# Fills of the first attention spread by their cost, the next stage's turns and products drawn in, and the recurrence's steps reordered, in a two-block kernel on one Trainium2 core

## The chip, the cores and the metric
One core of one Trainium2 chip runs the whole program. The metric is the device time of one execution, in microseconds (us). Engines are PE (TensorE), DVE (VectorE), ACT (ScalarE), POOL (GpSimd) and SP (SyncE, which here issues nearly all loads). Each works through its own instructions in order and waits on semaphores.

## What is computed
`reference` runs two blocks of two layers on 512 latent tokens of width 1024, all in 32-bit floats, with 256 context tokens beside them in the first block. The change touches the first block alone:
```python
def ab_layer(...):                       # layer 0: attention beside a short convolution
    q, k, v, g_a, xb, b_g, c_g, g_b = split_cols(modulate(x, shift, scale) @ w_in, widths)
    o_a = window_attention(q, k, v, kc, vc, sink)        # context: context_attention
    o_b = b_g * short_conv(c_g * xb, conv_w)
    y = concatenate([o_a * silu(g_a), o_b * silu(g_b)]) @ w_out
    x_new = layer_norm(ALPHA * x + gate * y, ln_g, ln_b)
def hgrn2(...):                          # layer 1: S_t = diag(f_t) S_{t-1} + k_t v_t^T, both directions
    k, log_f = sigmoid(-z), log_sigmoid(z)               # o_t = S_t^T q_t, decays by cumulative sums
```
The conditioning `mod = silu(c) @ w_ada[l] + b_ada[l]` gives shift, scale and gate of each layer; it depends on no token.

## The kernel before
Weights come in chunks of 1 MB through three slots (WSLOTS = 3): SP issues the load of chunk n when PE has released chunk n-3. Products that must be exact in 32 bits are made of three faster ones: ACT rounds a chunk to `weights_hi` (`hi_upto`), POOL subtracts to `weights_lo` (`lo_upto`, in the chunk's own slot), and PE multiplies hi by hi, hi by lo and lo by hi. PE's results go to three PSUM banks in turn (`ring`, `take`): a result needs the bank of the third result before it, as released by DVE ("v") or ACT ("a"). Products of the recurrence go to two further banks.

**First attention** (209.7 to 463 us). 48 units (6 query tiles, 8 heads) run in pairs: scores of both (PE), maxima (DVE), exponentials (ACT), scaling (DVE), turns (PE), their copies (one ACT, one DVE), values (PE). Between scaling and turns PE gets a fill from `AB_FILL`: 24 units of the branch beside the attention (bg, xb, cg; 2 chunks each; 24 matmuls of 512 or 256 columns), one a place over places 0 to 31; then six conditioning chunks of layer 1 (`mod_rows`, `mod_turn`) at places 32 to 37, beside which DVE makes the convolution; then ten of the 16 units of the output product (`y_unit`) at 38 to 47. At the fourth conditioning chunk SP reloads x and ctx (3 MB) in the same queue as the weights. ACT calls `hi_upto` for the next chunk inside a fill.

**Between the layers** (481.3 to 545.7). The context's output product yc0.0 to yc0.3; layer norm of four latent tiles on DVE, whose square root is ACT's `ln_root(1)`, behind `hi_upto("yc0.3")`; `join_part` of yc0.t between its tiles; then `ln_root(2)` for the context; six more conditioning chunks (`mod_run(1, 6, 12)`); turns h1.0 to h1.5 of the normed tiles, which ACT and DVE modulate; the gate row.

**Recurrence** (545.7 to 1122.5). First eight products (z, q, i of head pair 0), then eight steps: head pair hb, direction d = 0 or 1. A step on PE: `dg` (keys by queries, of which DVE keeps the diagonal), `kt` (turns of the decayed keys, which wait for DVE's `hg_ks`), level 0, product slot 0, `su` (state updates), level 1, slot 1, level 2, slot 2, `oi` (states by queries), and levels 3 to 6 with slots 3 to 6 behind them, slot 7 last. In even steps slots 0 to 4 hold products for the next step or head pair (5), in odd ones and the seventh step slots 0 to 5 (6). A level (16 matmuls of 64 columns) needs POOL's `level_args`, ACT's `level_exp` and DVE's `level_operand`. For the next step DVE makes |z| (`abs_z`, behind `across`), ACT exponential and logarithm, DVE `log_f_and_sums` with its scans, all ahead of DVE's operand of level 5; for d = 1 POOL then subtracts (`exclusive`, L2793) before ACT's `state_factors`.

## Time and profile before
| | |
|---|---|
| three runs | 2453.39, 2460.62, 2463.84 us, median 2460.62 |
| the profiled execution's own time | 2457.86 us |
| its span in the profile | 2456.1 us |
| mean granted clock of PE | 0.948 |
| instructions | 27907 |

The span runs from the first to the last instruction recorded; 1.8 us of the execution lie outside it. PE is busy for 91% of the span. From 1122.5 us on (out-projection, second block) nothing is edited.

### The profile page before, as it was taken

Reading aid. Unit: us, or ns where it says so; the run is one execution under the profiler, and the core shown is the slowest. Engines: PE = TensorE matmul, PEld = TensorE weight load, DVE = VectorE, ACT = ScalarE, POOL = GpSimd, SP = SyncE. Lnnn points to the kernel's source line nnn. Section 1 sums busy time; section 2 is a strip of 40 time slices with the busy share of each in tenths; the row PEclk is TensorE's granted clock in tenths of the full one; section 3 lists DMA queues with packets and bytes.
Section 4 is the critical chain, followed back from the end, with each engine's and each line's share of the span. In section 5 each row is a group of like instructions: output and inputs, shape, how many; then the busy total and the mean of one; then the engine's idle time right before and its main releaser. Section 6 shows DMA issues by size and latency. Waiting matters only on the chain. (4 is left out here: it accounts for less than half of the span.)

```text
span 2456.1 us, 27907 instructions
## 1 busy us (share of the span) xinstructions
PE 2243.3 (91%) x11655; PEld 1798.7 (73%) x11655; DVE 1104.9 (45%) x1647; ACT 668.0 (27%) x1030; POOL 835.7 (34%) x393
## 2 busy tenths in 40 slices
PE   5989996978999999999798878999998999999998
PEld 3768885856676767787665667888887767888886
DVE  2023557652556556556996553111116783111113
ACT  3222223223444444453111333010003163010111
POOL 1322102410323323223800024554554345454553
PEclk7999997979999999999899988999999999999999
DMA  9321115351101011112121012332322222232322
GB/s 296 83 72 52 35 35 172 79 163 52 35 23 47 18 35 35 35 52 78 42 65 35 35 35 70 102 103 86 103 92 97 86 86 69 86 103 88 101 95 77
DMA packets 173212, 187.45 MB, mean 76 GB/s; under 512 B 25552, under 2 KB 151840, under 8 KB 172960
## 3 DMA queue, kind: packets, MB, share of 16 engines
q1 hardware_dynamic: 165520, 178.56, 23.1%
q10 hardware_dynamic: 6992, 5.01, 0.7%
q8 instruction: 93, 1.52, 0.3%
q0 software_dynamic: 576, 2.10, 0.2%
q14 instruction: 31, 0.25, 0.0%
HBM read 183.56 MB, written 2.10 MB: 76 GB/s over the span
## 5 line engine op out<-in xcount | busy, mean ns | idle before, releaser
L2816 POOL TENSOR_TENSOR weights_lo<-weights_raw,weights_hi 128x2048 fp32r<-128x2048 f32 (+1 forms) x104 | 471.0, 4528 | 849.5 <-ACT weights_hi L1334 637.6
L646 PE MATMUL ring<-input_hi,weights_hi 128*128 128x512 f32 x784 | 305.4, 390 | 0.0
L648 PE MATMUL ring<-input_hi,weights_lo 128*128 128x512 f32 x784 | 305.0, 389 | 0.0
L647 PE MATMUL ring<-input_lo,weights_hi 128*128 128x512 f32 x784 | 305.0, 389 | 0.0
L2653 DVE CAST weights_hi<-weights_raw 128x2048 fp32r<-128x2048 f32 (+1 forms) x72 | 88.8, 1233 | 378.6 <-PE ring L648 173.9
L2807 POOL TENSOR_TENSOR h_w<-h_p 128x512 f32<-128x512 f32 x56 | 70.3, 1256 | 448.1 <-PE ring L935 367.6
L908 PE MATMUL obank<-acts,weights_raw 128*128 128x512 f32 x384 | 175.2, 611 | 0.8 <-issue 0.8
L646 PEld LDWEIGHTS ring<-input_hi,weights_hi 128*128 128x128 f32 x784 | 147.2, 188 | 31.1 <-issue 0.5
L648 PEld LDWEIGHTS ring<-input_hi,weights_lo 128*128 128x128 f32 x784 | 147.2, 188 | 30.6
L647 PEld LDWEIGHTS ring<-input_lo,weights_hi 128*128 128x128 f32 x784 | 147.2, 188 | 30.5 <-issue 0.2
L919 PE MATMUL obank<-weights_raw,acts 128*128 128x256 f32 x640 | 145.4, 387 | 0.0
L935 PEld LDWEIGHTS ring<-h_w 128*128 128x128 f32 x896 | 114.9, 205 | 32.7 <-issue 19.7
L1246 PE MATMUL ring<-weights_hi,hidden_hi 128*128 128x512 f32 x352 | 136.9, 389 | 0.0
L1247 PE MATMUL ring<-weights_lo,hidden_hi 128*128 128x512 f32 x352 | 136.9, 389 | 0.0
L1248 PE MATMUL ring<-weights_hi,hidden_lo 128*128 128x512 f32 x352 | 136.9, 389 | 0.0
L908 PEld LDWEIGHTS obank<-acts,weights_raw 128*128 128x128 f32 x384 | 73.6, 196 | 86.5 <-issue 86.4
L935 PE MATMUL ring<-h_w 128*128 128x64 f32 x896 | 116.1, 286 | 22.2 <-DVE h_w L2138 8.6
L919 PEld LDWEIGHTS obank<-weights_raw,acts 128*128 128x128 f32 x640 | 122.6, 194 | 17.1 <-issue 0.5
L2674 DVE TENSOR_TENSOR f_gate<-f_gate,ring 128x1024 f32<-128x1024 f32 x22 | 26.9, 1221 | 210.9 <-PE ring L648 210.9
L2921 POOL TENSOR_TENSOR hidden_lo<-f_gate,hidden_hi 128x1024 fp32r<-128x1024 f32 x22 | 52.6, 2390 | 160.8 <-ACT hidden_hi L1786 160.8
L1556 ACT ACTIVATE h_w<-h_w 128x1024 f32<-128x1024 f32 x56 | 59.0, 1056 | 147.6 <-POOL h_w L2808 147.5
L646 PE MATMUL ring<-ab_in_hi,weights_hi 128*128 128x512 f32 (+1 forms) x224 | 78.9, 352 | 17.3 <-POOL ab_in_lo L2823 9.5
(457 smaller groups left out, 4459.2 us busy)
## 6 DMA issues: line engine op xcount, KB each, us to landing
weights_raw<-in_w_ada SPq DMA_DIRECT2D x24, 1024.0 KB, 7.2
weights_raw<-in_ffn_w_gate SPq DMA_DIRECT2D x22, 1024.0 KB, 5.2
weights_raw<-in_ffn_w_up SPq DMA_DIRECT2D x22, 1024.0 KB, 5.2
weights_raw<-in_w_in_c SPq DMA_DIRECT2D x20, 1024.0 KB, 5.1
weights_raw<-in_ffn_w_down SPq DMA_DIRECT2D x16, 1024.0 KB, 4.9
weights_raw<-in_w_in_ab SPq DMA_DIRECT2D x9, 1024.0 KB, 5.2
weights_raw<-in_ev_w_in SPq DMA_DIRECT2D x8, 1024.0 KB, 5.8
weights_raw<-in_od_w_in SPq DMA_DIRECT2D x8, 1024.0 KB, 5.8
```

The lines of the kernel that those rows point to most:

```text
L646: pe.matmul(o, hi[:, k, ms], xh[:, k, t0:t0 + n], start=k == 0, stop=False)
L647: pe.matmul(o, hi[:, k, ms], xl[:, k, t0:t0 + n], start=False, stop=False)
L648: last = pe.matmul(o, lo[:, k, ms], xh[:, k, t0:t0 + n], start=False, stop=k == KD - 1)
L908: last = pe.matmul(ps[:, 0:L], wv[:, k, part * P:(part + 1) * P], HT[:, k, 0:L], start=k == 0, stop=k == KD - 1)
L919: last = pe.matmul(ps[:, j * WC:(j + 1) * WC], HT[:, k, t * P:(t + 1) * P], wv[:, k, :], start=k == 0, stop=k == KD - 1)
L935: last = pe.matmul(ps[:, j * 64:(j + 1) * 64], wt, rv[:, :, 1 - d, :], start=True, stop=True)
L1246: pe.matmul(o, F_HI[f // 2][:, f % 2, ts], hi[:, k, :], start=f == 0, stop=False, skip_group_check=True)
L1247: pe.matmul(o, F_HI[f // 2][:, f % 2, ts], lo[:, k, :], start=False, stop=False, skip_group_check=True)
L1248: last = pe.matmul(o, F_LO[f // 2][:, f % 2, ts], hi[:, k, :], start=False, stop=end, skip_group_check=True)
L2653: dve.tensor_copy(w_hi[:, 0:kt, :], WR[:, slot, 0:kt, :]).then_inc(done, 1)
L2807: pool.tensor_tensor(w4[:, :, :, 0, :], ref, p4[:, :, :, 0, :], ALU.subtract)
L2816: pool.tensor_tensor(W_LO[slot][:, 0:kt, :], WR[:, slot, 0:kt, :], w_hi[:, 0:kt, :], ALU.subtract).then_inc(sem("w_lo"), 1)
```

## The change
- `AB_FILL` is built from a list with a cost for each unit and put at the 24 even places, several units to a place. Conditioning chunks 0 to 8 (nine, MOD_FIRST = 9) stand one behind each weight chunk. Worked out from the code, the places read: bg 0 to 10, xb 12 to 22, cg 24 to 32, the y units from 34; conditioning chunks at 4, 10, 16, 22, 28, 34, 38, 42, 46. At 28: last unit of cg0, chunk 4, first of cg1. At 34: `x_again`, chunk 5, y(0,0). At 38: chunk 6, y(1,0). At 42: y(1,3), chunk 7, y(2,0). At 46: y(2,3), chunk 8, y(3,0). Three y units are left behind the attention.
- The convolution part follows each cg unit on DVE. x and ctx are reloaded from ACT's queue in five transfers (`x_again`). `y_hi` moves into the fills. `hi_upto("y0.0")` comes at the first unit of cg1.
- Between the layers `ln_root(1)` stands ahead of `hi_upto("yc0.3")`; h1.0 to h1.3 come before the last three conditioning chunks, and the first two z products before h1.4, h1.5 and the gate row.
- In the recurrence `dg` is made once a head pair, in the odd step behind `su`, from the sum of both directions' keys (`keys_of_both`). The product slots are 0, 1, 2, 4, 7 (five) or 0, 1, 2, 3, 5, 7 (six); the last step keeps its own. For d = 1 the scans yield the exclusive sums, and POOL's `exclusive` goes. The query operand moves out of `state_operands`. Before step 0 ACT takes only i(0,0) ahead of `state_factors(0)`.

```diff
-            return units + [None] * (8 - len(units))
+            places = range(8) if st == LAST else (0, 1, 2, 4, 7) if len(units) == 5 else (0, 1, 2, 3, 5, 7)
+            placed = dict(zip(places, units))
+            return [placed.get(i) for i in range(8)]
...
-        AB_STEPS = 32
+        Y_UNITS = [("y", c, t) for c in range(4) for t in range(TL)]
+        Y_AFTER = Y_UNITS[-3:]
+        MOD_FIRST = 9
+        a_woven = []
+        for nm, c, x, m in AB_UNITS:
+            a_woven.append((nm, c, x, m))
+            if (nm, c, x) == ("cg", 1, 1):
+                a_woven += [("y_hi", 2 * m), ("y_hi", 2 * m + 1)]
+            if (nm, c, x, m) == ("cg", 1, 1, 1):
+                a_woven.insert(-2, ("x_again",))
+            if (x, m) == (1, 1):
+                a_woven.append(("mod", sum(u[0] == "mod" for u in a_woven)))
+        for unit in Y_UNITS[:-3]:
+            a_woven.append(unit)
+            if unit[2] == TL - 1:
+                a_woven.append(("mod", sum(u[0] == "mod" for u in a_woven)))
+        a_woven.append(("last_mod",))
...
+        def fill_cost(unit):
+            if unit[0] in ("y_hi", "last_mod", "x_again"):
+                return 0
+            return 2 * KD if unit[0] == "mod" else 3 * KD * (2 if unit[0] != "y" and unit[2] == 0 else 1)
...
+        A_PLACES = 24
+        a_costs = [fill_cost(u) for u in a_woven]
         AB_FILL = {}
-        for u, unit in enumerate(AB_UNITS):
-            AB_FILL[u * AB_STEPS // len(AB_UNITS)] = unit
-        MOD_FIRST = 6
-        for j in range(MOD_FIRST):
-            AB_FILL[AB_STEPS + j] = ("mod", j)
-        Y_UNITS = [("y", c, t) for c in range(4) for t in range(TL)]
-        Y_WOVEN = 48 - AB_STEPS - MOD_FIRST
-        for u in range(Y_WOVEN):
-            AB_FILL[AB_STEPS + MOD_FIRST + u] = Y_UNITS[u]
-        Y_AFTER = Y_UNITS[Y_WOVEN:]
-        mod_no = {}
+        for u, unit in enumerate(a_woven):
+            place = min(A_PLACES - 1, A_PLACES * (2 * sum(a_costs[:u]) + a_costs[u]) // (2 * sum(a_costs)))
+            AB_FILL.setdefault(2 * place, []).append(unit)
...
                     if unit[1]:
                         mod_turn(1, unit[1] - 1)
                     mod_rows(1, unit[1])
+                    return
+                if unit[0] == "last_mod":
+                    mod_turn(1, MOD_FIRST - 1)
+                if unit[0] in ("y_hi", "last_mod", "x_again"):
                     return
                 if unit[0] == "y":
                     y_unit(*unit[1:])
...
                 last.then_inc(filled, 1)
                 used_with_unit()
+            for t in range(TL):
+                pe.wait_ge(sem("x1_ready"), t + 1)
+                turn_tiles("h1.", X, (t,), "va"[t % 2])
             mod_run(1, MOD_FIRST, 12)
...
                 return
-            for t in range(6):
-                pe.wait_ge(sem("x1_ready"), t + 1)
-                turn_tiles("h1.", X, (t,), "va"[t % 2])
-            gate_rows(1, 1)
-            pe.wait_ge(*read_of("h1.4"))
-            pe.wait_ge(*read_of("h1.5"))
+            pe.wait_ge(*read_of("h1.2"))
+            pe.wait_ge(*read_of("h1.3"))
...
-            for kind in "zqi":
+            product(("z", 0, 0))
+            product(("z", 0, 1))
+            for t in (4, 5):
+                pe.wait_ge(sem("x1_ready"), t + 1)
+                turn_tiles("h1.", X, (t,), "va"[t % 2])
+            gate_rows(1, 1)
+            pe.wait_ge(*read_of("h1.4"))
+            pe.wait_ge(*read_of("h1.5"))
+            product(("z", 0, 2))
+            for kind in "qi":
                 for part in range(C_PARTS[kind]):
...
-                K_, Q_, I_ = HK[b], HQ[q], HI[q]
+                Q_, I_ = HQ[q], HI[q]
...
-                pe.wait_ge(sem("hg_k"), st + 1)
-                pe.wait_ge(*product_emptied(("q", hb, 1)))
-                ps = take(f"dg{st}", "v")
-                for j in range(TL * HH):
-                    ch, h = divmod(j, HH)
-                    last = pe.matmul(ps[:, j * P:(j + 1) * P], K_[:, h, ch * P:(ch + 1) * P],
-                                     Q_[:, h, ch * P:(ch + 1) * P], start=True, stop=True)
-                last.then_inc(filled, 1)
...
+                    last.then_inc(filled, 1)
+                if d:
+                    pe.wait_ge(*product_emptied(("q", hb, 1)))
+                    pe.wait_ge(sem("hg_k_both"), hb + 1)
+                    ps = take(f"dg{st}", "v")
+                    for j in range(TL * HH):
+                        ch, h = divmod(j, HH)
+                        last = pe.matmul(ps[:, j * P:(j + 1) * P], HK[0][:, h, ch * P:(ch + 1) * P],
+                                         Q_[:, h, ch * P:(ch + 1) * P], start=True, stop=True)
                     last.then_inc(filled, 1)
...
                     sp.wait_ge(*released[n - WSLOTS])
-                if n == mod_no[1, 3]:
-                    sp.wait_ge(*fill_of("cg1.11"))
-                    sp.dma_start(X[:, 0:TL, :], a["x"][0].rearrange("(t p) n -> p t n", p=P)).then_inc(sem("x_in"), 16)
-                    sp.dma_start(X[:, TL:6, :], a["ctx"][0].rearrange("(t p) n -> p t n", p=P)).then_inc(sem("x_in"), 16)
...
                 ts = slice(qt * P, (qt + 1) * P)
-                act.wait_ge(sem("conv"), 8)
+                act.wait_ge(sem("conv"), 6 if qt < TL else 8)
                 act.wait_ge(sem("A_normed"), qt + 1)
...
-                    if unit[1] == MOD_FIRST - 1:
-                        hi_upto("y0.0")
+                elif unit[0] == "last_mod":
+                    mod_columns(1, MOD_FIRST - 1)
+                elif unit[0] == "x_again":
+                    act.wait_ge(*fill_of("cg1.11"))
+                    for c in range(4):
+                        cs = slice(c * WC, (c + 1) * WC)
+                        act.dma_start(X[:, 0:TL, cs], a["x"][0][:, cs].rearrange("(t p) n -> p t n", p=P)).then_inc(sem(f"x_again{c}"), 16)
+                    act.dma_start(X[:, TL:6, :], a["ctx"][0].rearrange("(t p) n -> p t n", p=P)).then_inc(sem("ctx_again"), 16)
+                elif unit[0] == "y_hi":
+                    y_hi(unit[1])
                 elif unit[0] == "y":
-                    if unit[1:] == (0, 0):
-                        mod_columns(1, MOD_FIRST - 1)
                     if unit[2] == 0:
                         hi_upto(f"y0.{unit[1] + 1}" if unit[1] < 3 else "yc0.0")
-                elif unit[2:] == (0, 0) and unit[:2] != ("cg", 1):
-                    hi_upto(names[names.index(f"{unit[0]}{unit[1]}") + 1])
-            attention("A", APB, APT, 0.125, True, lambda i: y_hi(i - 36) if 36 <= i < 40 else None, woven)
+                elif unit[2:] == (0, 0):
+                    hi_upto((names + ["y0.0"])[names.index(f"{unit[0]}{unit[1]}") + 1])
+            attention("A", APB, APT, 0.125, True, lambda i: None, woven)
             for qt in range(4, 6):
                 y_hi(qt)
             for unit in Y_AFTER:
                 woven(unit)
-            hi_upto("yc0.3")
...
-            ln_root(1, 0, 4)
-            ln_root(2, 4, 6)
-            mod_run(1, MOD_FIRST, 12)
-            for t in (1, 3, 5):
+            def h1_tile(t):
                 act.wait_ge(*fill_of(f"h1.{t}"))
                 j = 0 if t < TL else 1
                 for k in range(KD):
                     ins = act.activation(HT[:, k, t * P:(t + 1) * P], bank(f"h1.{t}")[:, k * P:(k + 1) * P], ACT.Identity,
...
                 ins.then_inc(emptied["a"], 1)
+            hi_upto("yc0.2")
+            ln_root(1, 0, 4)
+            hi_upto("yc0.3")
+            h1_tile(1)
+            h1_tile(3)
+            mod_run(1, MOD_FIRST, 12)
+            ln_root(2, 4, 6)
...
-            act.wait_ge(*fill_of("gate1.0"))
-            ps = bank("gate1.0")
-            act.activation(GT[:, 0, :], ps[:, :], ACT.Copy).then_inc(emptied["a"], 1)
...
                     act.wait_ge(sem("hg_w"), 7 * (st - 1))
+                if st >= 2 and st % 2 == 0:
+                    act.wait_ge(*fill_of(f"dg{st - 1}"))
...
-                    act.wait_ge(sem("hg_excl"), STEPS[st][0] + 1)
...
-            for part in range(3):
-                take_product(("z", 0, part))
+            take_product(("z", 0, 0))
+            take_product(("z", 0, 1))
+            h1_tile(5)
+            act.wait_ge(*fill_of("gate1.0"))
+            ps = bank("gate1.0")
+            act.activation(GT[:, 0, :], ps[:, :], ACT.Copy).then_inc(emptied["a"], 1)
+            take_product(("z", 0, 2))
             keys(0)
             log1p_exp(0)
             for part in range(2):
                 take_product(("q", 0, part))
-            for part in range(3):
-                take_product(("i", 0, part))
+            take_product(("i", 0, 0))
             state_factors(0)
             level_exp(0)
             level_exp(1)
+            take_product(("i", 0, 1))
+            take_product(("i", 0, 2))
...
-                if unit[0] == "mod":
-                    if unit[1] < 4:
-                        for x in range(2):
-                            conv_part(unit[1], x)
+                if unit[0] in ("mod", "y_hi", "last_mod", "x_again"):
                     return
                 if unit[0] == "y":
                     _, c, t = unit
-                    if c == 0 and t == 0:
-                        dve.wait_ge(sem("x_in"), 64)
+                    if t == 0:
+                        dve.wait_ge(sem(f"x_again{c}"), 16)
                     join_part(f"y0.{c}.{t}", c, t, 1, ATMP)
                     return
...
                 dve.wait_ge(*read_of(label))
+                if nm == "cg":
+                    conv_part(i, x)
...
+            dve.wait_ge(sem("ctx_again"), 16)
             layer_norm(1, "x1", 0, 4, 32, lambda t: join_part(f"yc0.{t}", t, 4, 2, ATMP))
+            modulated(1, "h1.", (0, 2))
             layer_norm(2, "x1", 4, 6, 32)
...
-            modulated(1, "h1.", (0, 2, 4))
+            modulated(1, "h1.", (4,))
...
-                for h in range(HH):
-                    dve.tensor_tensor_scan(HP[b][:, h, 0:L], tab("chunk"), HT_[b][:, h, 0:L], 0.0, ALU.mult, ALU.add)
-                    last = dve.tensor_tensor_scan(HP[b][:, h, L:LT], tab("chunk", 0, LC), HT_[b][:, h, L:LT], 0.0, ALU.mult, ALU.add)
-                link(last)
-                link(dve.tensor_copy(PL[b], HP[b][:, :, :].rearrange("p h (c t) -> p h c t", t=P)[:, :, :, P - 1]))
+                ends = [v[:, :, :].rearrange("p h (c t) -> p h c t", t=P)[:, :, :, P - 1] for v in (HP[b], HT_[b])]
+                if STEPS[st][1] == 0:
+                    for h in range(HH):
+                        dve.tensor_tensor_scan(HP[b][:, h, 0:L], tab("chunk"), HT_[b][:, h, 0:L], 0.0, ALU.mult, ALU.add)
+                        last = dve.tensor_tensor_scan(HP[b][:, h, L:LT], tab("chunk", 0, LC), HT_[b][:, h, L:LT], 0.0, ALU.mult, ALU.add)
+                    link(last)
+                    link(dve.tensor_copy(PL[b], ends[0]))
+                else:
+                    if st == 1:
+                        dve.memset(HP[b][:, :, 0:1], 0.0)
+                        link(dve.memset(HP[b][:, :, L:L + 1], 0.0))
+                    for h in range(HH):
+                        dve.tensor_tensor_scan(HP[b][:, h, 1:L], HT_[b][:, h, 0:L - 1], tab("chunk", 1, L), 0.0, ALU.add, ALU.mult)
+                        last = dve.tensor_tensor_scan(HP[b][:, h, L + 1:LT], HT_[b][:, h, L:LT - 1], tab("chunk", 1, LC), 0.0, ALU.add, ALU.mult)
+                    link(last)
+                    link(dve.tensor_tensor(PL[b], ends[0], ends[1], ALU.add))
                 dve.tensor_copy(DEC[b], PL[b]).then_inc(sem("hg_sums"), 1)
...
             def state_operands(st):
-                b, q = st % 2, STEPS[st][0] % 2
+                b = st % 2
                 dve.wait_ge(sem("hg_k"), st + 1)
                 dve.wait_ge(sem("hg_exps"), st + 1)
                 dve.tensor_tensor(HZ[b][:, :, :], HZ[b][:, :, :], HK[b][:, :, :], ALU.mult).then_inc(sem("hg_ks"), 1)
+            def query_operand(st):
+                b, q = st % 2, STEPS[st][0] % 2
                 dve.wait_ge(*product_emptied(("q", STEPS[st][0], 1)))
                 dve.tensor_tensor(HT_[b][:, :, 0:L], HT_[b][:, :, 0:L], HQ[q][:, :, :], ALU.mult).then_inc(sem("hg_qi"), 1)
...
                 dve.wait_ge(*fill_of(f"dg{st}"))
                 src = bank(f"dg{st}")[:, :].rearrange("p (j c) -> p j c", j=TL * HH)
-                idb = IDENT.unsqueeze(1).to_broadcast([P, TL * HH, P])
-                S = HSC[hb % 2]
-                if d == 0:
-                    dve.tensor_tensor(S[:, :, :], src, idb, ALU.mult).then_inc(emptied["v"], 1)
-                    dve.wait_ge(*read_of(f"dg{st}"))
-                else:
-                    dve.tensor_tensor(HDG[:, :, :], src, idb, ALU.mult).then_inc(emptied["v"], 1)
-                    dve.wait_ge(*read_of(f"dg{st}"))
-                    link(dve.tensor_tensor(S[:, :, :], S[:, :, :], HDG[:, :, :], ALU.add))
+                own = IDENT.bitcast(U32).unsqueeze(1).to_broadcast([P, TL * HH, P])
+                dve.copy_predicated(HSC[STEPS[st][0] % 2][:, :, :], own, src).then_inc(emptied["v"], 1)
+                dve.wait_ge(*read_of(f"dg{st}"))
+            def keys_of_both(hb):
+                k0, k1 = HK[0][:, :, 0:L], HK[1][:, :, 0:L]
+                dve.wait_ge(sem("hg_k"), 2 * hb + 2)
+                dve.tensor_tensor(k0, k0, k1, ALU.add).then_inc(sem("hg_k_both"), 1)
...
+                dve.wait_ge(*product_emptied(("q", hb, 1)))
                 level_operand(7 * st)
-                diagonal(st)
                 level_operand(7 * st + 1)
+                if d:
+                    keys_of_both(hb)
                 level_scores(st, 0)
                 if d == 0 and hb:
                     inside(hb - 1)
+                query_operand(st)
                 states(st)
+                if d:
+                    diagonal(st)
...
                         lo_upto("y10.0")
                     if more:
-                        exclusive(st + 1)
                         pool.wait_ge(sem("hg_sums"), st + 2)
```

## Rows read from the trace of the kernel before

**Rows 1.** The page, busy time of each engine over the span.
```profile
PE 2243.3 (91%) x11655; PEld 1798.7 (73%) x11655; DVE 1104.9 (45%) x1647; ACT 668.0 (27%) x1030; POOL 835.7 (34%) x393
```
**Rows 2.** Windows: stretch, length, busy us of PE, PEld, DVE, ACT, POOL; clock, DMA.
```profile
209.70:378.00 168.30, 158.74 (x1289) 136.85 (x1288) 92.36 (x219) 49.31 (x103) 22.94 (x5) 1.00 0.13 42
378.00:420.00 42.00, 22.84 (x200) 14.66 (x197) 33.32 (x70) 17.62 (x47) 7.07 (x3) 0.65 0.77 239
420.00:481.30 61.30, 58.48 (x477) 54.97 (x478) 38.44 (x75) 14.12 (x30) 30.70 (x9) 0.96 0.21 53
481.30:545.70 64.40, 50.88 (x365) 42.13 (x364) 42.86 (x69) 20.52 (x49) 13.81 (x3) 0.79 0.59 180
...
870.00:936.60 66.60, 62.61 (x287) 44.82 (x287) 42.06 (x46) 30.30 (x35) 21.70 (x15) 0.90 0.10 32
936.60:999.20 62.60, 60.96 (x334) 49.78 (x335) 36.33 (x44) 26.17 (x36) 17.42 (x14) 1.00 0.11 34
```
**Rows 3.** Waits of PE, 209.7 to 545: total us, times, longest.
```profile
PE ring L707 <- ACT mod_rows L1357: 5.9, 1, 5.9
...
PE ring L821 <- DVE a_tmp L1894: 3.7, 2, 3.5
PE ring L740 <- ACT a_probs_t L1445: 2.7, 8, 0.3
```
**Rows 4.** Timeline of PE near 379 and 524: start, us, instruction.
```profile
379.10 1.07 PE L698 MATMUL ring<-weights_raw,silu_cond 128*32 128x256 f32 x16
...
524.28 1.93 PE L698 MATMUL ring<-weights_raw,silu_cond 128*32 128x256 f32 x16
...
527.09 1.93 PE L698 MATMUL ring<-weights_raw,silu_cond 128*32 128x256 f32 x16
```
**Rows 5.** DMA issues near 381 and 456: count, KB each, us to landing.
```profile
weights_raw<-in_w_ada SPq DMA_DIRECT2D x1, 1024.0 KB, 13.8
...
weights_raw<-in_w_out_ab SPq DMA_DIRECT2D x1, 512.0 KB, 5.1
```
**Rows 6.** Timeline of ACT, 482 to 524.
```profile
487.78 1.92 ACT L1334 ACTIVATE weights_hi<-weights_raw 128x2048 fp32r<-128x2048 f32 x1 [4.37 <-DMA weights_raw<-in_w_out_ab]
...
497.65 0.21 ACT L1481 ACTIVATE small<-small 128x4 f32<-128x4 f32 x1
520.01 0.20 ACT L1481 ACTIVATE small<-small 128x2 f32<-128x2 f32 x1 [22.16 <-DVE small L1907]
```
**Rows 7.** Timeline of PE at the recurrence's first step.
```profile
600.93 1.95 PE L984 MATMUL ring<-h_q,h_k 128*128 128x128 f32 x16
609.62 2.40 PE L993 MATMUL ring<-tables,h_z 128*128 128x128 f32 x10 [6.75 <-DVE h_z L2125]
613.18 3.65 PE L935 MATMUL ring<-h_w 128*128 128x64 f32 x16 [1.17 <-DVE h_scores L2149]
616.62 8.41 PE L908 MATMUL obank<-acts,weights_raw 128*128 128x512 f32 x16
```
**Rows 8.** Timeline of PE in the fifth and sixth steps.
```profile
905.31 7.09 PE L908 MATMUL obank<-acts,weights_raw 128*128 128x512 f32 x16
...
923.19 7.09 PE L935 MATMUL ring<-h_w 128*128 128x64 f32 x32 [2.14 <-DVE h_w L2138]
...
936.56 1.97 PE L935 MATMUL ring<-h_w 128*128 128x64 f32 x16 [1.85 <-DVE h_diag L2152]
...
975.35 1.89 PE L935 MATMUL ring<-h_w 128*128 128x64 f32 x16
...
999.22 1.97 PE L935 MATMUL ring<-h_w 128*128 128x64 f32 x16 [1.66 <-DVE h_scores L2149]
```
**Rows 9.** Timeline of DVE in the same two steps.
```profile
908.24 1.52 DVE L2138 TENSOR_TENSOR h_w<-h_w,h_q 128x512 f32<-128x512 f32 x1
...
919.22 3.91 DVE L2138 TENSOR_TENSOR h_w<-h_w,h_q 128x512 f32<-128x512 f32 x1
...
982.33 0.68 DVE L2138 TENSOR_TENSOR h_w<-h_w,h_k 128x512 f32<-128x512 f32 x1
```

More of the change, by code:

```diff
@@ L226, in program @@
         HKT = [view(gt_at + D, 4 * HH, P, name="h_kt"), view(xc + 1280, HH, P, name="h_kt")]
-        HDG = view(bc_at + D, TL * HH, P, name="h_diag")
         HO = view(hi_at, TL, D, name="h_out")
@@ L490, in program @@
                   22: ("ev", 1, 3), 26: ("em", 0), 28: ("em", 1), 30: ("em", 2)}
+        E_FILL = {i: [unit] for i, unit in E_FILL.items()}
         E_WOVEN = 3
@@ L691, in mod_rows @@
             def mod_rows(l, j):
-                mod_no[l, j] = len(chunks)
                 wv = chunk(cols(a["w_ada"][l], j * WC))
@@ L733, in attention @@
                     if what == "fill":
-                        fill(FILLS[kind][i])
+                        for unit in FILLS[kind][i]:
+                            fill(unit)
                     elif what == "scores" and i % 2 == 0:
@@ L828, in y_unit @@
                 if t == 0:
-                    if c == 0:
-                        mod_turn(1, MOD_FIRST - 1)
                     parts_of["y", c] = split_chunk(f"y0.{c}", head_rows(c))
@@ L1420, in attention @@
                     if what == "fill":
-                        fill(FILLS[kind][i])
+                        for unit in FILLS[kind][i]:
+                            fill(unit)
                     elif what == "scores":
@@ L2034, in attention @@
                     if what == "fill":
-                        fill(FILLS[kind][i])
+                        for unit in FILLS[kind][i]:
+                            fill(unit)
                     elif what == "scores":
```

7 lines of the change are left out of this document (removed).

## The prediction
> **What bounds the kernel now.** I read the page first: PE is busy 91% of the span [rows 1], no other engine comes near half. So the time is PE's work, its idle time, and stretches in which it works at the lower clock. Next I read windows over the three edited places [rows 2]. In the attention PE idles 9.6 us up to 378, 19.2 in 378:420, 2.8 after: 31.5 in all. The middle window, where the conditioning chunks stand in a row, has a clock of 0.65 and DMA engines busy for 0.77: it waits for weights. Between the layers (481:546) it idles 13.5 at a clock of 0.79. In the recurrence PE is nearly full: step 4 (870 to 936.6) idles 4, step 5 1.6. Then the waits [rows 3]: 5.9 and 3.5 us are single waits between the layers, the 0.3 us waits those of the attention's pairs. Last the timelines [rows 4, 6 to 9], to see what is late behind each wait.
>
> The sum is made against the profiled execution's own time, 2457.86; the median of three is 2.76 above. In the timelines an operation's duration overlaps the next by 0.15 to 0.2 (a level at 613.18 lasts 3.65, the product behind starts at 616.62 [rows 7]), so I take a level as 1.75 at full clock and 3.5 at half, a product as 6.95 and, begun at the low clock, 8.2.
>
> **A. Attention, 209.7 to 481.3.** Three more conditioning chunks come in: 1.07 of products at full clock [rows 4] and about 0.4 of turns, 1.5 each, +4.5. The idle of before goes: -31.5. Its low clock goes: a clock of 0.65 over 22.8 busy us is 8, the 0.96 later 2.3, and some 1.7 of turns: -12.
>
> New stalls: ACT's `hi_upto` for the next chunk is called in the fill directly behind a conditioning chunk (places 28, 34, 38, 42, 46). That load needs the slot three chunks back, which the last unit of the weight chunk before releases, and at these five places that unit stands in the same fill or the one just ahead. So the load starts while ACT already waits for it, and ACT's exponentials and copies for the pair are queued behind. A 512 KB piece takes 5.1 [rows 5]; with two issues ahead of the last piece I estimate 1.3 more, 6.4; `hi` 1.92 [rows 6] and ACT's copies of the pair follow. Less what PE has of its own in the fill: 2.6 at 28, 5.4 at 38, 6.5 at 42, 3.3 at 46. At 34 the 3 MB of x and ctx run beside it from ACT's queue. The rows give two bounds for the load: 6.4 alone, 13.8 for a chunk that landed behind the same 3 MB [rows 5]. Two queues sharing lie between; I take the middle, 10.1, and the stall is 7.5 (3.8 to 11.2). Sum +25.3. Each stall is followed by low clock over some 2 to 2.5 us of lost work; five make +11 (bounds 0 and 17, were each to cost one operation of 7 at 8.2 and two levels at 3.5). In the fills without stall each pair still waits about 0.34 for ACT's `a_probs_t`, as 8 pairs do now [rows 3]; 19 more: +6.5. Moving the convolution parts behind the cg units adds nothing to DVE, which is busy 92 of 168 us here [rows 2]; would it not hide, 8 parts would go on the pairs' maxima. A: 4.5 - 31.5 - 12 + 25.3 + 11 + 6.5 = **+3.8**.
>
> What the row shows of the shared load is only a chunk behind 3 MB in one queue, 13.8 [rows 5]. The Trainium skill (DMA: Bandwidth & Descriptors, "Queues, rings and completion order") says that an engine takes turns between its queues packet by packet; by this estimate the chunk would take about 9.4 and the stall 0.7 less. No row of before has two such queues side by side.
>
> **B. Between the layers.** `ln_root(1)` now stands behind a `hi` that needs a chunk in the middle of the row; before, it stood behind `hi` of yc0.3, whose load came 4.37 late [rows 6]. DVE's statistics of the norm are done near 489, the root ran at 497.65; I put it at 490.9, so the normed tiles come 6.8 earlier. With it go PE's waits of 5.9 and 3.5 [rows 3]: -9.4. Three conditioning chunks leave the row where they cost 2.8 each (524.28 to 527.09 [rows 4]): -8.4. Low clock beside them: -2.4. New: h1.2 waits for the join of yc0.3, h1.3 for the bank that DVE frees behind h1.0: estimated 4.8, between 0 (DVE keeps pace) and 9.4 (the wait only changes its name). The context's tiles h1.4, h1.5 stand behind two z products of 7 each, which cover `ln_root(2)` (520.01, after 22 us of waiting for DVE [rows 6]); without that cover it would be some 6. B: -9.4 - 8.4 - 2.4 + 4.8 = **-15.4**.
>
> **C. Start of the recurrence.** ACT takes i(0,0) alone before `state_factors(0)`, so DVE's operand is there near 596 where PE needs it at 601. The waits of 6.75 and 1.17 go [rows 7], `dg` of step 0 (1.95, 1.8 net) goes, and the low clock that follows the wait: `kt` 1.1, level 0 1.8, product 1.3. C: **-13.9**.
>
> **D. The steps.** I walk step 4 with the slots 0, 1, 2, 4, 7. PE reaches level 4 at 905.3 (no product in slot 3), but DVE's operand ends at 909.8 [rows 8, 9]: an idle 4.5. Then level 4 at the low clock 3.5, product 8.2, levels 5 and 6 3.5, product 6.95, `kt` 1.1: the next level 0 at 933.1, where it was 936.56 [rows 8]. That is -3.5; the old wait of 2.14 and the low clock of the two levels (7.09 for both [rows 8]) are in it, and the gone subtraction on POOL, beside which DVE's 0.68 took 3.91 [rows 9]. Steps 0 and 2 walked in the same way give -2.4 and -3.1. Together -9.0.
>
> Step 5 has the slots 0, 1, 2, 3, 5, 7. Level 5 stands right behind level 4, PE is free at 977.1, the operand of level 5 ends at 983.0 [rows 8, 9], because |z| and the scans of the next step still stand ahead of it: an idle 5.9. Then level 3.5, product 8.2, level 1.75, product 6.95, `kt` 1.1: 1004.5 instead of 999.22, +5.3. Its `dg` stays, 1.8, and level 1 waits 0.4 for the bank of `su`; the product after level 0 no longer meets a low clock, -1.0 on average. So +6.5, three times: +19.5. The seventh step has the wait of step 5 and no `dg`: -0.5; the last keeps its slots and has its `dg`, 1.8 + 0.4: +2.2. D: -9.0 + 19.5 - 0.5 + 2.2 = **+12.2**. The sum of keys (one DVE operation of about 0.7), `copy_predicated` for a product and the shifted scans (same lengths) lie beside PE's products and are costed at nothing; were the cover gone, they would be 0.7 a step. ACT's `keys` of the next even step now waits for `dg` of the odd step; `dg` is made in the first third of the step and the keys are made in its second half, so nothing is late behind it.
>
> **Sum.** +3.8 - 15.4 - 13.9 + 12.2 = -13.3: 2444.6 for the profiled execution, **2447** against the median.
>
> **Rivals.**
> *Slower: clock lost behind each empty slot.* Where levels stand without a product between them, the clock stays low not for one level but through the next and its product. For it: the two levels at 923.19 took 7.09, both at half speed after a wait of only 2.14 [rows 8]. Against it: in step 5 the same order of work keeps a clock of 1.00 [rows 2]. It would add one level and most of a product, about 4 us, in each of seven steps: +28, 2475. The change is slower than before from +1.9 a step, by over 0.5% from +3.7. The Trainium skill (TensorE: Matmul & The Clock Gate, Part 1) says that micro-idles between groups of matmuls make the clock swing between its two levels; by that this rival would hold.
>
> *The attention's fills do not stall.* If the slot is released soon enough, or the load is less than 6.4, the 25.3 and 8 of the 11 of low clock go: 2414. For it: in the first 168 us, with the same calls of `hi_upto`, PE idles just 9.6 [rows 2]. Against: there no conditioning chunk takes a slot in between.
>
> *The shifted slots are better than walked.* The next step's chain starts earlier because products come earlier in ACT's order, and the operand of level 5 with it. The odd steps' idle and low clock go (19) and half of the even steps' idle (6): 2422. Against: DVE's order before level 5 is the same.
>
> *No change.* The root stays as late as before since `hi_upto("yc0.2")` itself waits for its load; B loses its 9.4: 2457.
>
> **How the numbers follow.** Forecast 0.45, its own range 2439 to 2455 (the bounds of the load at 34, of the low clock and of the 4.8). Slower rival 0.12, no stalls 0.15, better slots 0.13, no change 0.15. The range reaches to 2418, between the two faster rivals, and to 2468, short of the slower one; outside lie about two thirds of 0.15 and of 0.12. A measurement of this kernel tells about 0.5% (12.3 us) from no change. Faster than 2448.3 are the two fast rivals (0.28) and somewhat over half of the forecast (0.25): 0.53. Slower than 2472.9: most of the slow rival (0.11) and 0.03 of the forecast's tail: 0.14. Within: 0.33.
>
> **What would show it.** A: in the changed profile ACT waits for DMA of the weights at places 28, 34, 38, 42 and 46, 3 to 8 us of PE idle at each, and no stretch with a clock of 0.65 for 40 us. If PE idles under 15 there, the load term is wrong. B: `ln_root(1)` within 9 us of the last y unit; the 5.9 is absent. If ACT still waits over 4 for a load ahead of the root, the fourth rival holds. C: `kt` begins directly behind the third i product. D: PE waits on `h_w` before level 4 in even steps (4 to 5) and before level 5 in odd ones (about 6); four `dg` instead of eight; nothing of L2793 on POOL. Even steps under 63.1, odd ones near 69. If the levels behind the empty slots take 3.5 each and the product behind them 8 or more in all steps, the slower rival holds. The prediction would be wrong above all if several conditioning chunks wait at PE itself for their load, which I cost at nothing, since the slot of each is free well before its place.

## The result and the profile after

Four runs of the changed kernel, beside four of the kernel before: 2478.80 us median (2477.32 to 2484.11) against 2460.46 (2453.39 to 2463.84), ratio 1.0089, 95% interval 1.0072 to 1.0106. The change makes the kernel slower by 0.9%. 2447 with a range of 2418 to 2468 was predicted. The profiled span went from 2456.1 to 2477.4, +21.3.

The page's busy times, the row that answers [rows 1]:
```profile
PE 2234.0 (90%) x11591; PEld 1791.5 (72%) x11591; DVE 1086.7 (44%) x1645; ACT 667.8 (27%) x1029; POOL 826.8 (33%) x389
```
PE is busy 9 us less and the span is 21 longer, so its idle time rose by 31. Windows of the changed kernel (columns as in [rows 2]); the second ends where the three y units behind the attention are done, as 481.3 did before, the third behind the third z product, as 566.5 did:
```profile
209.70:378.00 168.30, 151.99 (x1265) 130.22 (x1264) 100.46 (x224) 51.21 (x110) 22.80 (x5) 0.98 0.23 70
378.00:514.60 136.60, 96.41 (x754) 86.23 (x755) 59.27 (x138) 33.06 (x80) 36.98 (x11) 0.81 0.31 85
514.60:588.40 73.80, 63.80 (x374) 47.63 (x373) 47.16 (x72) 20.44 (x42) 13.80 (x3) 0.88 0.38 115
```
The attention's stretch takes 304.9 us instead of 271.6, +33.3; PE idles 56.5 of them, 31.5 before, and is busy 248.4, 240.1 before. The stretch between the layers takes 73.8 instead of 85.2, -11.4. What PE waited for from 209 to 560, total us, times, longest, against [rows 3]:
```profile
PE ring L759 <- ACT a_probs_t L1471: 38.6, 20, 12.7
PE obank L781 <- ACT a_probs_t L1471: 5.2, 1, 5.2
PE obank L781 <- issue: 3.9, 2, 2.3
PE ring L707 <- DVE a_tmp L1933: 3.7, 2, 2.9
PE obank L781 <- DVE a_probs_t L2113: 3.1, 2, 2.4
```
The 5.9 us of ACT's `mod_rows` is gone. The largest waits are now for ACT's copy of the turned probabilities. The longest case, place 34, in the timelines of PE and of ACT (start, us, instruction, idle before it in brackets with what ended it):
```profile
426.01 1.22 PE L759 MATMUL ring<-a_kv,a_q 64*128 64x128 f32 x8 [12.66 <-ACT a_probs_t L1471]
```
```profile
412.42 0.38 ACT L1382 ACTIVATE mod_rows<-ring 128x256 f32<-128x256 f32 x1
423.69 1.91 ACT L1359 ACTIVATE weights_hi<-weights_raw 128x2048 fp32r<-128x2048 f32 x1 [10.89 <-DMA weights_raw<-in_w_out_ab]
425.50 0.37 ACT L1471 ACTIVATE a_probs_t<-ring 128x256 f32<-128x256 f32 x1
```
ACT stands 10.9 us at `hi_upto("y0.1")`, and a copy of 0.37 us, for which PE waits, is queued behind it. The five waits of this kind are 6.2, 12.7, 5.7, 7.2 and 5.2 us (places 28, 34, 38, 42, 46). The load's issues from 407 to 411 (count, KB, us to landing):
```profile
resid<-in_x ACTq DMA_DIRECT2D x4, 512.0 KB, 7.3
resid<-in_ctx ACTq DMA_DIRECT2D x1, 1024.0 KB, 14.6
weights_raw<-in_w_out_ab SPq DMA_DIRECT2D x2, 256.0 KB, 9.8
weights_raw<-in_w_out_ab SPq DMA_DIRECT2D x1, 512.0 KB, 13.9
```
Between the layers and at the start of the recurrence, PE's timeline of the changed kernel. Its last two rows answer [rows 7]: `kt` has no wait, `dg` is gone:
```profile
542.85 1.06 PE L707 MATMUL ring<-tables,resid 128*128 128x128 f32 x8 [0.79 <-DVE a_tmp L1933]
546.81 1.94 PE L707 MATMUL ring<-tables,resid 128*128 128x128 f32 x8 [2.90 <-DVE a_tmp L1933]
550.22 1.94 PE L707 MATMUL ring<-tables,resid 128*128 128x128 f32 x8 [1.46 <-DVE acts L1924]
...
559.41 17.05 PE L927 MATMUL obank<-acts,weights_raw 128*128 128x512 f32 x32 [1.15 <-DMA weights_raw<-in_w_in_c]
...
622.67 1.26 PE L1013 MATMUL ring<-tables,h_z 128*128 128x128 f32 x10
623.77 1.90 PE L954 MATMUL ring<-h_w 128*128 128x64 f32 x16
```
And one odd and one even step, against [rows 8]:
```profile
858.18 1.90 PE L954 MATMUL ring<-h_w 128*128 128x64 f32 x16
865.90 3.67 PE L954 MATMUL ring<-h_w 128*128 128x64 f32 x16 [5.83 <-DVE h_w L2193]
869.38 8.82 PE L938 MATMUL obank<-weights_raw,acts 128*128 128x256 f32 x32
878.03 1.90 PE L954 MATMUL ring<-h_w 128*128 128x64 f32 x16
...
925.86 3.67 PE L954 MATMUL ring<-h_w 128*128 128x64 f32 x16 [4.34 <-DVE h_w L2193]
929.33 9.53 PE L927 MATMUL obank<-acts,weights_raw 128*128 128x512 f32 x16
938.70 3.68 PE L954 MATMUL ring<-h_w 128*128 128x64 f32 x32
```
The waits foretold, 5.9 before level 5 and 4.5 before level 4, stand there as 5.83 (four times) and 4.34 (three times).

The whole difference by stretch: attention +33.3; between the layers -11.4; from there to the first level 0 -11.3 (35.4 instead of 46.7); from it to the last level +14.0 (521.3 instead of 507.3); the unedited rest -3.3. Sum +21.3. No run tries the edits between the layers by themselves; their -11.4 is read from these windows.

### The profile page after: what moved, and what is told of

Same layout as the page of the kernel before. It is cut to its first block and busy times, and to the rows that moved or that the text cites. A ratio compares the mean times of both kernels' runs of the same rounds, so it can differ in the third digit from the quotient of the medians.

```text
span 2477.4 us, 27765 instructions
## 1 busy us (share of the span) xinstructions
PE 2234.0 (90%) x11591; PEld 1791.5 (72%) x11591; DVE 1086.7 (44%) x1645; ACT 667.8 (27%) x1029; POOL 826.8 (33%) x389
```

## The experiments

The theory after the result: the attention's loss comes from ACT waiting for a load that was issued only a few us before, and the recurrence's from the empty slots. Each ratio is to runs of the kernel before made beside it (medians 2456.9 to 2460.2).

**Old slots.**
```diff
-            places = range(8) if st == LAST else (0, 1, 2, 4, 7) if len(units) == 5 else (0, 1, 2, 3, 5, 7)
+            places = range(8)
```


> The changed kernel with the recurrence's product slots as they were (0 to 4, or 0 to 5); all else stays. Theory (the empty slots cost: PE waits 4.34 before level 4 in three even steps and 5.83 before level 5 in four odd ones, and runs a level and a product at the low clock behind each): those waits go, some 2 us come back before levels 5 and 6 of the even steps, and the recurrence becomes shorter than before by 5 to 15 us instead of longer by 17. Expected 2452 us, 2446 to 2457. Rival (the time is lost to the new order of dg, keys and scans, not to the slots): 2476 to 2482.


Measured 2463.58, ratio 1.0021 (1.0012 to 1.0030): 15.2 us off the changed kernel, where 27 were expected. The seven waits of 4.3 and 5.8 us went, but behind the even steps 0, 2 and 4 the next `kt` now waits 4.3 to 4.5:
```profile
800.64 3.68 PE L954 MATMUL ring<-h_w 128*128 128x64 f32 x32
808.62 2.39 PE L1013 MATMUL ring<-tables,h_z 128*128 128x128 f32 x10 [4.29 <-DVE h_z L2176]
811.17 1.11 PE L954 MATMUL ring<-h_w 128*128 128x64 f32 x4 [0.16 <-DVE h_w L2193]
```
The slots are a cause, the rival falls. But of the even steps only step 0 gets shorter (56.6 for 60.4 from `kt` to `kt`); steps 2 and 4 take 62.4 and 64.1, in the changed kernel 62.4 both, since PE gets to `kt` sooner and waits there for the keys. And in steps 2, 4, 6 and 7 level 0 now waits 2.3 us for its operand, with low clock behind it:
```profile
877.56 3.27 PE L954 MATMUL ring<-h_w 128*128 128x64 f32 x16 [2.26 <-DVE h_w L2193]
880.62 9.21 PE L927 MATMUL obank<-acts,weights_raw 128*128 128x512 f32 x16
```

**ACT rounds one unit later.**
```diff
-                    if unit[2] == 0:
+                    if unit[2] == 1:
                         hi_upto(f"y0.{unit[1] + 1}" if unit[1] < 3 else "yc0.0")
-                elif unit[2:] == (0, 0):
+                elif unit[2:] == (0, 1):
```


> The changed kernel, but ACT rounds the next weight chunk one unit later (at the second unit of a chunk and not at its first). Theory (ACT stands in front of a load that was issued only some 2 us before, and the pair's exponentials and copies are queued behind it): of the 36.9 us of PE waits at places 28, 34, 38, 42 and 46 at least 30 go, and some 8 of low clock with them. Expected 2440 us, 2434 to 2448. Rival (the loads are late for PE too, so that the wait moves to the next chunk's first product): 2470 or more, with new waits on weights_lo in the attention.


Measured 2450.41, ratio 0.9969 (0.9954 to 0.9984): 28.4 off the changed kernel. PE's waits from 209 to 486:
```profile
PE obank L781 <- DVE a_probs_t L2113: 10.4, 6, 2.9
PE ring L759 <- ACT a_probs_t L1471: 7.1, 20, 0.6
PE obank L781 <- issue: 4.1, 3, 2.3
```
```profile
209.70:485.60 275.90, 246.60 (x2039) 214.47 (x2037) 163.95 (x364) 84.24 (x190) 60.33 (x16) 0.96 0.30 85
```
All five long waits are gone and none on `weights_lo` over 1.4 took their place; the attention fell from 304.9 to 275.9. That settles the mechanism. 10 us are short of the expectation: PE's idle time fell by 27.2 (56.5 to 29.3) and not by the 36.9 of the five waits, because others grew, DVE's copies from 3.1 to 10.4; and PE's busy time fell by 1.8, where some 8 of low clock were expected.

**x in quarters**, each ahead of its output chunk, ctx at the end:
```diff
+                if unit[0] == "y" and unit[2] == 2:
+                    if unit[1] < 3:
+                        x_columns(unit[1] + 1)
+                    else:
+                        act.dma_start(X[:, TL:6, :], a["ctx"][0].rearrange("(t p) n -> p t n", p=P)).then_inc(sem("ctx_again"), 16)
...
                     act.wait_ge(*fill_of("cg1.11"))
-                    for c in range(4):
...
+                    x_columns(0)
```


> The changed kernel, but x is reloaded one quarter at a time (0.5 MB ahead of each output chunk) and ctx at the end, in place of 3 MB at once at place 34. Theory (two queues share the engines, so the chunk for y0.1 took 15.2 us from issue to landing beside 3 MB): the chunk lands in 7 to 9 us, the wait of 12.7 at place 34 falls to 5 or 6, the others stay. Expected 2471 us, 2467 to 2474. Rival (the chunk is late because of the conditioning chunk issued just ahead, not of x): 2476 to 2482.


Measured 2469.99, ratio 1.0046 (1.0031 to 1.0061), 8.8 off. Issues near place 34, and PE's wait there:
```profile
weights_raw<-in_w_out_ab SPq DMA_DIRECT2D x2, 256.0 KB, 4.0
weights_raw<-in_w_out_ab SPq DMA_DIRECT2D x1, 512.0 KB, 5.0
```
```profile
415.69 0.84 PE L759 MATMUL ring<-a_kv,a_q 64*128 64x128 f32 x8 [4.19 <-ACT a_probs_t L1471]
```
The last piece landed after 5.0 instead of 13.9 and the wait is 4.2 instead of 12.7: the 3 MB make most of it, not the conditioning chunk, which still stands ahead.

**x in one queue with the weights**, the same five transfers issued by SP directly ahead of the chunk for y0.1 and no longer by ACT:
```diff
+                if n == split_chunks[split_no["y0.1"]]:
+                    sp.wait_ge(*fill_of("cg1.11"))
+                    for c in range(4):
...
+                    sp.dma_start(X[:, TL:6, :], a["ctx"][0].rearrange("(t p) n -> p t n", p=P)).then_inc(sem("ctx_again"), 16)
```


> The changed kernel with its five reloads of x and ctx in SP's queue, directly ahead of the chunk for y0.1, instead of in ACT's queue beside it. Theory (two queues side by side move less: 257 GB/s on average over 408 to 424.3 in the changed kernel, with 180 to 290 in the middle where both are at work, and 340 to 420 with one): 4 MB at some 370 GB/s take 11.5 us, the chunk lands near 420 in place of 423.7, the wait at place 34 falls from 12.7 to 9 or 10, time 2476 us, 2472 to 2479. Rival (the transfers of x are slow in either queue, or the chunk gains from sharing): the chunk lands at 424 or later, the wait is 12 or more, time as the changed kernel's or above.


Measured 2482.39, ratio 1.0102 (1.0081 to 1.0123). The last piece landed 13.2 us after its issue at 410.2, at 423.4 (423.7 in the changed kernel). But x was issued 1.5 us earlier here (405.93 against 407.45), so the chunk landed 17.5 us after the first transfer of x where it took 16.2, and PE's wait is longer:
```profile
425.74 1.22 PE L759 MATMUL ring<-a_kv,a_q 64*128 64x128 f32 x8 [16.36 <-ACT a_probs_t L1477]
```
The rival holds: sharing between two queues is not what costs. What the 4 MB lack is rate: 240 GB/s in one queue (405.9 to 423.4) and 251 in two (407.5 to 424.2). Why the last 5 us before 421 move only 163 to 248 GB/s here, where 340 to 420 flowed from 412 to 416, stays open. It may be in part the chunk's own: with nothing beside it, in the kernel with x in quarters, it moved 216 GB/s in its middle (410 to 411.5). The chunk behind 3 MB in the kernel before ([rows 5], 13.8) was one of `w_ada`, and it moved at 328 to 365.

**All three edits.**


> The three edits together on the changed kernel: old slots, ACT's rounding one unit later, x reloaded in quarters. Theory: the gains of the first two add (27 and 39), of the third most is already in the second. Expected 2411 us, 2403 to 2420, faster than before by 1.6 to 2.3 per cent. Rival (the waits are one chain and the gains overlap, or DVE becomes late in the attention): 2430 or more.


Measured 2434.81, ratio 0.9894 (0.9874 to 0.9915): 44 off the changed kernel, 25 faster than before. The attention takes 271.0 us with three conditioning chunks more than before:
```profile
209.70:480.70 271.00, 244.56 (x2027) 212.35 (x2025) 162.80 (x364) 84.59 (x190) 60.40 (x16) 0.96 0.29 86
```
The sum of the three gains is 52.4, so 8 are missing, and the time is the rival's (2430 or more). Up to the last level of the recurrence, where no unedited part enters, the traces say the same: 16.3, 31.5 and 12.9 us for the single edits, 60.7 in all, and 51.6 for the three together (1093.4 against 1145.0). The gains overlap by 9: beside the first two, x in quarters brings 3.8 and not 12.9, as the theory had it: with the rounding later, the wait at place 34 is gone already. The unedited rest is no part of this: over the thirteen profiled kernels it varied from 1332 to 1340, and the changed kernel's own was the shortest.

**The recurrence alone**, on the kernel before: all edits from the last i product on, with shifted and with old slots; and **the shifted slots alone** on the kernel before.


> The kernel before with the change's edits from the last i product on alone (order before step 0, dg once a head pair, exclusive scans, shifted slots); attention and the stretch between the layers as before. Theory (the parts add; in the changed kernel's trace the start of the recurrence is 11.3 us shorter and the steps 13.9 us longer, 3.1 of low clock counted in the steps): 2463 us, 2459 to 2467. Rival (the steps depend on how they are reached, so that the parts do not add): outside of that.

> The same without the shifted slots. Theory: the start keeps its 11.3 us, the steps are as long as in the run with old slots, 2.3 us under those of before, so 2447 us, 2443 to 2451; dg once a head pair saves three dg of 1.8 us, and kt then waits for its keys instead (4.3 to 4.5 in each even step). Rival (dg once saves what it weighs): 2441 or less.

> The kernel before with the shifted slots alone. Theory (each odd step waits 5.8 us before level 5 and runs a level and a product at the low clock; in even steps the wait only changes its place): slower by 12 to 20 us, 2476 us. Rival (the shift costs only beside the new order of dg and keys): within 5 us of before.


Measured 2462.51 (ratio 1.0019, 1.0008 to 1.0030), 2445.49 (0.9948, 0.9932 to 0.9964) and 2492.29 (1.0140, 1.0122 to 1.0158). The first two came as expected: the parts add. The third was off: the shift alone costs 34.9, twice the expectation. Worked out from the starts of `kt` in the traces (us from one `kt` to the next):

| kernel | steps 0 to 6 | first `kt` to last level |
|---|---|---|
| before | 64.9, 63.3, 64.3, 64.9, 66.4, 62.8, 68.6 | 510.8 |
| slots alone | 68.7, 70.0, 65.5, 70.5, 68.9, 70.8, 75.5 | 542.5 |
| new order, shifted slots (changed) | 60.4, 70.6, 62.4, 70.7, 62.4, 70.7, 70.9 | 522.4 |
| new order, old slots | 56.6, 66.1, 62.4, 66.7, 62.4, 67.0, 64.9 | 504.7 |

The third row is the changed kernel, whose attention differs too, but the steps do not feel it: the recurrence alone gives 522.7 for its 522.4. The fourth is the recurrence alone. The new order (`dg` once, no `exclusive`) is worth 20 us under the shifted slots and 6 under the old ones. Part of it is seen in step 6 of the slots alone, PE and DVE:
```profile
1080.71 3.68 PE L937 MATMUL ring<-h_w 128*128 128x64 f32 x16 [9.13 <-DVE h_w L2140]
```
```profile
1076.15 0.69 DVE L2140 TENSOR_TENSOR h_w<-h_w,h_k 128x512 f32<-128x512 f32 x1
1076.75 3.91 DVE L2140 TENSOR_TENSOR h_w<-h_w,h_q 128x512 f32<-128x512 f32 x1
```
POOL's `exclusive` runs beside the second operation, from 1076.3 to 1080.1, and it takes 3.91 ([rows 9] has the same); in the recurrence alone, without `exclusive`, it takes 0.69. With old slots a product covers most of it, and PE waits 2.14 [rows 8]; with an empty slot PE waits 9.13 instead of 5.83. The odd steps are 5.6 to 8 us longer, step 6 is 6.9 and the other even ones are 1.2 to 3.8; what makes up the even steps' part beyond this operation was not tried by itself.

**The convolution behind the copies**, on the kernel with three edits: DVE keeps the part in a list and makes it after it has copied the pair's turned probabilities:
```diff
                 if nm == "cg":
-                    conv_part(i, x)
+                    conv_later.append((i, x))
...
                         dve.tensor_copy(PT[:, i % 2, 0:nb * P], ps[:, 0:nb * P]).then_inc(emptied["v"], 1)
+                        while conv_later:
+                            conv_part(*conv_later.pop(0))
```


> The kernel with all three edits, and each convolution part moved on DVE behind the copy of the pair's turned probabilities. In the kernel with three edits PE waits 9.4 us, 6 times, for DVE's copy of the turned probabilities, at the places of the cg units. Theory (DVE does the convolution first, and the copy is queued behind it): those waits go, some low clock with them, 2424 us, 2420 to 2430. Rival (the convolution then delays the next pair's maxima and the wait only moves): 2432 to 2438.


Measured 2432.01, ratio 0.9894 (0.9875 to 0.9914), the ratio of the kernel with three edits. The rival holds: the convolution is what makes DVE late, and it does so in either place. PE's waits from 209 to 486 have changed their names:
```profile
PE ring L768 <- DVE a_probs L2114: 6.6, 2, 5.1
PE ring L716 <- ACT a_probs L1457: 4.1, 1, 4.1
PE obank L781 <- DVE a_probs_t L2122: 3.5, 3, 2.5
PE ring L878 <- ACT a_probs L1457: 3.0, 1, 3.0
```
With the parts behind the copies it is the next pair's maxima and scaling that come late, where it was the copies before.

**Factors first**, on the kernel with three edits:
```diff
                 level_exp(7 * st + 6)
-                between(4)
                 if more:
                     state_factors(st + 1)
+                between(4)
```


> The kernel with three edits, and in each step ACT's state_factors for the next step ahead of its taking the product of slot 4. In the kernel with three edits the sums for step 3 are ready at 762.9, but ACT begins the factors at 765.9, behind the product of slot 4, and kt waits 4.29 us for what follows from them. Theory: kt's wait falls by 2 to 3 us in each of four even steps, and the low clock behind it in part: 2425 us, 2421 to 2430. Rival (ACT's factors delay the product's bank or the level exponentials by as much): 2433 to 2437.


Measured 2423.42, ratio 0.9866 (0.9841 to 0.9891). ACT and PE at the end of step 2, first in the kernel with three edits, then here:
```profile
765.28 0.60 ACT L1551 ACTIVATE h_q<-obank 128x512 f32<-128x512 f32 x1 [1.86 <-PE obank L927]
765.90 1.28 ACT L1582 ACT_TABLE_LOAD   x1
767.19 0.21 ACT L1582 ACTIVATE small<-small 128x12 f32<-128x12 f32 x1
```
```profile
773.06 2.39 PE L1013 MATMUL ring<-tables,h_z 128*128 128x128 f32 x10 [4.29 <-DVE h_z L2183]
```
```profile
760.54 0.21 ACT L1582 ACTIVATE small<-small 128x12 f32<-128x12 f32 x1 [0.82 <-DVE small L2177]
```
```profile
768.46 2.40 PE L1013 MATMUL ring<-tables,h_z 128*128 128x128 f32 x10 [2.09 <-DVE h_z L2183]
```
ACT's exponentials begin as soon as DVE's sums are there, with no copy and no table load (1.28 us, between two functions) ahead of them, and `kt`'s wait falls from 4.29 to 2.09. Up to the last level 8.5 us are gained. This is the fastest kernel of the study, 34.7 us under the kernel before.

**All five.**


> Three edits, the convolution behind the copies, and the factors first. Theory: the two gains add, 2414 us, 2408 to 2422. Rival (one of the two does nothing): 2423 or more.


Measured 2427.74, ratio 0.9880 (0.9859 to 0.9901). The rival holds. The convolution's place adds nothing, as it did alone; the median is even 4.3 above factors first, but the runs overlap (2424.89 to 2431.39, 2421.15 to 2427.58).

## Why the prediction was wrong

**A is the step that failed: +3.8 predicted, +33.3 measured.** The stalls that it named came, by its mechanism, at the five places. What failed is the size of three terms: the stalls (11.6 us short), the idle time that was to go (13.1 short) and the low clock that was to go (4.8 short).
- Stalls, 25.3 predicted, 36.9 measured. By place: 28, 2.6 and 6.2; 34, 7.5 and 12.7; 38, 5.4 and 5.7; 42, 6.5 and 7.2; 46, 3.3 and 5.2. At 34 I took the middle between 6.4 and 13.8 for the load. It took 13.9 for the last piece and 15.3 from the first issue, past the upper bound: the chunk lands with the end of the 3 MB (423.7, 424.2), not halfway. The estimate that I drew from the Trainium skill (DMA: Bandwidth & Descriptors, "Queues, rings and completion order"), 9.4, was further off still. The trace agrees with the turns: from 413 to 417.5 the two queues moved 543 and 506 packets. But both together moved 230 GB/s there, where the chunk behind 3 MB in the kernel before moved at 328 to 365, so the turns did not bring it in sooner. At 28 the last piece took 8.6 behind the conditioning chunk issued 1.4 us before it, where I had 5.1.
- The rest of the idle, 6.5 predicted, 19.6 measured (56.5 less 36.9). I subtracted all of the 31.5 us of before and gave back one kind of wait, the small ones for ACT's copies. Those came as forecast, 6.9. The other 12.7 are waits that I had at nothing: DVE's copies 4.0, DVE's taking of the fills' results 3.1, ACT's of the conditioning 1.2, 3.9 for which the profile shows no cause, and smaller ones. The convolution was costed at nothing; with the stalls out of the way, DVE's late copies are 10.4 us, and the one other place tried for it cost the same. The sentence that named where it would fall if the cover were gone was there, but without a price, and nothing of it entered the sum or the range.
- Low clock and busy time: 243.6 us of PE's work predicted (240.1 + 4.5 - 12 + 11), 248.4 measured. The clock of 378:514.6 is 0.81, which over 96 busy us is 18, reckoned as I reckoned the 8 of before. But not much of it hangs on the five stalls: without them, with ACT rounding later, PE is still busy 246.6 at a clock of 0.96. So it is less the 11 that were too few than the 12 of before that did not go; PE still idles 29 us there, in shorter waits.

**B: -15.4 predicted, -11.4 measured.** The root came 10.1 us after the first context product began (524.69 against 514.6), 16.4 before, so 6.3 earlier where I had 6.8; the new waits of h1.1 to h1.3 are 5.15 for 4.8. What was missing is the clock behind them: the two z products took 17.05 where 13.97 was their time before, and a load is late by 1.15. My sign for the "no change" rival, ACT waiting over 4 us for a load ahead of the root, was there (4.35), and the rival did not hold: ACT was through with that chunk at 523.4, when DVE's statistics had only just ended (522.9), so the load cost the root 1.8 us at most.

**C and D.** Of the 13.9 in C, 3.1 are low clock behind the first level 0, which the boundary used above counts in the steps. Cut so, C is -10.8 predicted and -11.3 measured, D +9.1 predicted and +14.0 measured. The waits were right to 0.2 us (4.34 and 5.83 for 4.5 and 5.9), odd steps 70.7 for 69. Two things were short. The product behind the empty slot takes 8.6 to 9.4 from its start to the next instruction's instead of 8.2, seven times, 5.8 in all. And the seventh step, which I had 0.5 shorter, is 2.3 longer (70.9 for 68.6). Against them, even steps are 60.4 and 62.4, for 63.1 in step 4, and the last step grew by half a us for 2.2.

**The rivals.** "Slower, clock lost behind each empty slot" gave 2475, near the 2479 measured, but for a reason that is not there: after the wait one level and one product are slow, and the levels behind them run at full clock again (3.68 for two, 938.70 above), so that it adds to the walk 0.8 us a step, 6 of its 28. The swing between the two levels that the Trainium skill names for micro-idles (TensorE: Matmul & The Clock Gate, Part 1) is seen in this case's traces, behind waits of 2.1 and 2.3 us too: the two levels at 923.19 of the kernel before [rows 8], the level and product at 877.56 with old slots. It does not last as long as the rival had it. "No stalls" did not hold in the changed kernel; made true by moving ACT's rounding, it gave 2450, not 2414: the attention took 275.9 where this rival comes to 242.1, with 29.3 of idle for 6.5 and 246.6 busy for 235.6. "Better slots" was wrong: the operand's chain did not move. "No change" was wrong in its mechanism.

From -13.3 to +21.3 is 34.6: A 29.5 (11.6 stalls, 13.1 idle, 4.8 low clock), B 4.0, C -0.5, D 4.9, the rest -3.3. The range took the bounds of single terms (the load, the clock) and had none for its largest term, "-31.5 idle goes". Had 19.6 been left of it, with DVE busy 92 of 168 us [rows 2] a reason to, the forecast would have been near 2460; with the load at its upper bound and D as measured, near 2470. That is still short of 2479: no one term explains the miss.

## What to carry to other kernels

When a fill is moved between two weight chunks, look at who waits for the next chunk's load in program order, and what small thing is queued behind that wait: 0.37 us of copying behind a 10.9 us wait cost 12.7. Call the consumer of a load one unit later than the load can be issued, not in the same unit. And an idle sum taken from a stretch may be subtracted only wait by wait: what ended each must be gone in the new order, or it comes back under another name.

Where a chain between engines (here z, logarithm, scans, factors, keys) sets the step, moving matmuls about only moves the wait. Starting ACT's part of the chain before an unrelated copy was worth 8.5 us; the shifted slots on PE went 17 us the wrong way (2462.51 against 2445.49 for the recurrence alone).

## What the runs showed of the hardware

- A chunk of 1 MB issued behind or beside 3 MB landed about 15 us after its own first issue in either case (423.4 with one queue, 423.7 with two). Beside them, the two queues moved equal numbers of packets, at 230 GB/s together; alone, its last piece took 5.0 us.
- A wait of 4.3 or 5.8 us of PE is followed by one level at half clock (3.67 for 1.90) and a product of 8.7 to 9.6 us instead of 7.1; the levels behind them are at full clock. So such a wait costs about 3.4 to 4.3 us more than its length. Waits of 2.1 to 2.3 us can cost as much: 3.5 in the level and product at 877.56 with old slots (3.27 and 9.21 for 1.90 and 7.09), 3.4 in the two levels at 923.19 of the kernel before (7.09 for 3.68).
- A DVE operation of 0.69 us takes 3.91 while POOL subtracts over 1536 columns beside it (3.79); without a product to hide it, PE's wait was 9.13 where it is 5.83 without that subtraction.
- Instructions that no edit touched took from 1332 to 1340 us in thirteen profiled kernels; a gain of 7 us in the total can be lost or found there. So two kernels of this case are better compared up to the last edited instruction.
